# Three-pass split scores for the stick-breaking and the neighbourhood heads, with the sticks' low parts made on GpSimd

## The reference

```python
# stick-breaking: z = q k^T / 8, per block of 128 queries
log_beta = log_sigmoid(z)
log_1m = where(mask, log_sigmoid(-z), 0)
suffix = cumsum(log_1m, reverse) - log_1m
wts = where(mask, exp(log_beta + suffix), 0);  out = wts @ v
# neighbourhood: a grid of 8 rows by 64 columns; a query sees 16 columns of the 8 rows
p = softmax(q k^T / 8 + bias[row distance, column distance]);  out = p @ v
```

## Time and profile before

| | |
|---|---|
| runs | 1906.74, 1907.86, 1908.47 us, median 1907.86 |
| the profiled execution | 1907.13 us, span 1905.4 us from first to last instruction, mean granted clock 0.998 |
| TensorE, matmuls | 1890.5 us busy, 9126 instructions |
| DVE | 1072.6 us busy (56%) |
| ACT | 787.6 us busy (41%) |
| GpSimd | 159.3 us busy (8%) |
| stick stage | about 597 to 790 us from the start |
| neighbourhood stage | about 1539 to 1758 us |

### The profile page before, as it was taken

One profiled execution on the slowest core, in us unless ns is written; L12 is line 12 of the kernel. 1 busy time (PEld: TensorE's weight loads), 2 busy tenths in 40 slices (PEclk: granted clock), 3 DMA queues, 4 the chain that ended last, 5 costly groups with the idle time before them and its releaser, 6 DMA issues.

```text
span 1905.4 us, 25474 instructions
## 1 busy us (share of the span) xinstructions
PE 1890.5 (99%) x9126; PEld 1513.2 (79%) x9126; DVE 1072.6 (56%) x1719; ACT 787.6 (41%) x1261; POOL 159.3 (8%) x238
## 2 busy tenths in 40 slices
PE   9999999999999999999999999999999999999998
PEld 8888888888888777788888888876777887777777
DVE  7788534434456676654343446576676555655553
ACT  6576422222334444532222234255555344444442
POOL 3111000000000000000000000000002054532000
PEclk9999999999999999999999999999999999999999
DMA  7323332323232122223322232212313232322221
GB/s 249 115 93 121 100 98 91 114 84 99 95 100 77 60 66 66 79 91 97 110 99 82 94 111 88 67 45 62 95 56 92 83 95 79 91 78 89 77 93 68
DMA packets 50847, 173.78 MB, mean 91 GB/s; under 512 B 7456, under 2 KB 11680, under 8 KB 50768
## 3 DMA queue, kind: packets, MB, share of 16 engines
q1 hardware_dynamic: 44336, 162.62, 26.6%
q0 software_dynamic: 6432, 10.13, 2.1%
HBM read 168.51 MB, written 4.21 MB: 91 GB/s over the span
## 4 chain that ended last, share of the span: by engine, by line
PE 95%; DVE 2%; ACT 2%; issue 1%; DMA 1%; SPq 0%; DVEq 0%; ACTq 0%
PE ps L474 17%; PE ps L476 16%; PE ps L475 16%; PE sc L474 6%; PE sc L476 6%; PE sc L475 6%; PE tr L474 4%; PE tr L475 4%; PE tr L476 4%; PE ps L642 3%; PE tr L608 3%; PE sc L582 2%; PE ps L582 1%; PE sc L613 1%; PE ps L629 1%
## 5 line engine op out<-in xcount | busy, mean ns | idle before, releaser
L1020 ACT ACTIVATE Wh<-Wr 128x1024 fp32r<-128x1024 f32 (+2 forms) x268 | 300.2, 1120 | 642.6 <-PE ps L476 285.2
L474 PE MATMUL ps<-Hh,Wh 128*128 128x512 f32 x1136 | 465.7, 410 | 0.0
L476 PE MATMUL ps<-Hh,Wl 128*128 128x512 f32 x1136 | 444.3, 391 | 0.0
L475 PE MATMUL ps<-Hl,Wh 128*128 128x512 f32 x1136 | 443.1, 390 | 0.0
L1467 DVE TENSOR_TENSOR Wl<-Wr,Wh 128x1024 fp32r<-128x1024 f32 (+2 forms) x268 | 352.3, 1314 | 131.9 <-ACT Wh L1020 130.7
L474 PEld LDWEIGHTS ps<-Hh,Wh 128*128 128x128 f32 x1136 | 213.5, 188 | 56.8 <-issue 16.4
L476 PEld LDWEIGHTS ps<-Hh,Wl 128*128 128x128 f32 x1136 | 213.1, 188 | 47.0
L475 PEld LDWEIGHTS ps<-Hl,Wh 128*128 128x128 f32 x1136 | 213.9, 188 | 39.4 <-issue 0.5
L474 PE MATMUL sc<-Hh,Wh 128*128 128x512 f32 x432 | 168.6, 390 | 0.0
L475 PE MATMUL sc<-Hl,Wh 128*128 128x512 f32 x432 | 168.1, 389 | 0.0
L476 PE MATMUL sc<-Hh,Wl 128*128 128x512 f32 x432 | 168.1, 389 | 0.0
(11 more groups left out here) (307 smaller groups left out, 2639.7 us busy)
## 6 DMA issues: line engine op xcount, KB each, us to landing
Wr<-in_w SPq DMA_DIRECT2D x228, 512.0 KB, 3.5
Wr<-in_w SPq DMA_DIRECT2D x32, 768.0 KB, 4.3
Wr<-in_w SPq DMA_DIRECT2D x16, 640.0 KB, 3.9
scr<-in_rpb POOLq DMA_DIRECT2D x128, 24.0 KB, 2.1
X<-in_x SPq DMA_DIRECT2D x8, 256.0 KB, 4.4
Wr<-in_wri SPq DMA_DIRECT2D x4, 512.0 KB, 3.5
out_t<-X SPq DMA_DIRECT2D x8, 256.0 KB, 2.4
scr<-d_rel POOLq DMA_DIRECT2D x8, 192.0 KB, 3.6
```

What stands on the lines that cost most here:

```text
L474: pe.matmul(bank[:, 0:n], hi, rh[:, k, :], start=(k == 0), stop=False)
L475: pe.matmul(bank[:, 0:n], hi, rl[:, k, :], start=False, stop=False)
L476: return pe.matmul(bank[:, 0:n], lo, rh[:, k, :], start=False, stop=(k == kc - 1))
L1020: act.activation(place(Wh, slot, kc), place(Wr, slot, kc), ACT.Copy).then_inc(w_hi, 1)
```

## The change

1. Scores of the stick and neighbourhood pairs are split: for Q and K of the next pair there are high and low parts `Qh`, `Ql`, `Kh`, `Kl` in chunks 8 to 11 of `Yh` and `Yl`. ACT makes the high parts (`pair_hi`), 16 in each stage. The low parts are made by GpSimd for the sticks (a list of 16 in its program) and by DVE for the neighbourhood (`pair_lo`). `head` gets an argument `part`, and a chunk of scores is three products.
2. The group of scores is issued part by part, alternating between the heads; the 512-wide tile is one chunk; the wait on `nb_ok` stands behind the first part of head 0's wide tile.
3. At t = 0 TensorE waits for `qk_lo` in place of `taken`.
4. In `out_proj` of the sticks and of the recurrent block, units 4 and 5 come out of the loop and wait for the sums of units 0 and 1.
5. In the neighbourhood stage the last transposes go behind block 6 of unit 32, the last values behind block 1 of unit 33.

```diff
@@ -206,6 +206,8 @@
 
         QT, KT, VT, Vn = part(0, 2, S), part(1024, 2, S), part(2048, 2, S), part(3072, 2, S)
         Pb = part(4096, 4, S)
+        Qh, Ql, Kh, Kl = Yh[:, 8:10, :], Yl[:, 8:10, :], Yh[:, 10:12, :], Yl[:, 10:12, :]
+        pair_rows = {"q": (QT, Qh, Ql), "k": (KT, Kh, Kl), "qn": (QT, Qh, Ql), "kn": (KT, Kh, Kl)}
         PT = part(6144, 2, 4 * S)
         KT2 = part(10240, 2, S)
         ropes = part(11264, 2, S)
@@ -283,6 +285,7 @@
         t_s, t_nm, t_e, t_p, t_t, t_pt = (sem(n) for n in ("t_s", "t_nm", "t_e", "t_p", "t_t", "t_pt"))
         t_in, t_nr, nb_ok = sem("t_in"), sem("t_nr"), sem("nb_ok")
         t_av = sem("t_av")
+        qk_hi, qk_lo = sem("qk_hi"), sem("qk_lo")
         v_tp, v_ok = sem("v_tp"), sem("v_ok")
         sb_ok, yt_ok = sem("sb_ok"), sem("yt_ok")
         one_ok = sem("one_ok")
@@ -392,6 +395,13 @@
             for i in range(12, 16):
                 store_mem(i)
 
+            for n in range(8):
+                for tag in ("q", "k"):
+                    src, hi, lo = pair_rows[tag]
+                    pool.wait_ge(qk_hi, 2 * n + (1 if tag == "q" else 2))
+                    pool.tensor_tensor(lo[:, n % 2, :], src[:, n % 2, :], hi[:, n % 2, :].bitcast(F32), ALU.subtract)\
+                        .then_inc(qk_lo, 1)
+
             pool.wait_ge(t_p, STEP0["gqa"])
             pool.wait_ge(t_av, STEP0["gqa"] // 4)
             pool.dma_start(ropes, a["rope"]).then_inc(rope_in, 16)
@@ -525,7 +535,10 @@
                     if name == "rg_out":
                         unit(u0 + 2, CORNER, ps[2], kc, Yh, Yl)
                     unit(u0 + 3, 1, ps[3], kc, Yh, Yl)
-                    it0 = 2
+                    for m in range(2):
+                        pe.wait_ge(x_ok, x0 + m + 1)
+                        unit(u0 + 4 + m, m, ps[b0 + m], kc, Yh, Yl)
+                    it0 = 3
                 with pe.Fori(it0, 3 if name == "odd_out" else 4) as it:
                     for m in range(2):
                         pe.wait_ge(x_ok, 2 * it + (x0 + m - 1))
@@ -575,18 +588,38 @@
                 else:
                     wait(pe, t_e, g)
 
-                def head(t, h, c0, c1):
+                def head(t, h, c0, c1, part=None):
+
                     b, lo, hi = block_of(kind, t), 64 * h, 64 * h + 64
-                    k0 = key_chunks(kind, b)[0] * P
-                    keys = {GQA: KT[lo:hi, grp, c0:c1], WIN: KT2[lo:hi, grp, c0:c1]}.get(kind, KT[lo:hi, par, c0:c1])
-                    return pe.matmul(pair_bank(kind, t)[:, h, c0 - k0:c1 - k0], queries[lo:hi, b * P:(b + 1) * P], keys,
-                                     start=True, stop=True)
+                    k0, q = key_chunks(kind, b)[0] * P, slice(b * P, (b + 1) * P)
+                    out = pair_bank(kind, t)[:, h, c0 - k0:c1 - k0]
+                    if part is None:
+                        keys = {GQA: KT[lo:hi, grp, c0:c1], WIN: KT2[lo:hi, grp, c0:c1]}.get(kind, KT[lo:hi, par, c0:c1])
+                        return pe.matmul(out, queries[lo:hi, q], keys, start=True, stop=True)
+                    rows, keys = ((Qh, Kh), (Ql, Kh), (Qh, Kl))[part]
+                    return pe.matmul(out, rows[lo:hi, par, q], keys[lo:hi, par, c0:c1], start=(part == 0), stop=(part == 2))
 
                 def span(t):
                     cs = key_chunks(kind, block_of(kind, t))
                     return cs[0] * P, (cs[-1] + 1) * P
 
                 k0, k1 = span(t)
+                if kind in (STICK, NBR):
+                    for part in range(3):
+                        mm = head(t + 1, 0, *span(t + 1), part)
+                        if part == 2:
+                            mm.then_inc(nb_ok, 1)
+                        mm = head(t, 1, k0, k1, part)
+                    mm.then_inc(t_s, 2)
+                    for part in range(3):
+                        mm = head(t, 0, k0, k1, part)
+                        if part == 2:
+                            mm.then_inc(t_s, 2)
+                        if part == 0:
+                            pe.wait_ge(nb_ok, narrow)
+                        mm = head(t + 1, 1, *span(t + 1), part)
+                    mm.then_inc(nb_ok, 1)
+                    return
                 cuts = (k0, k0 + 256, k1) if k1 - k0 == S else (k0, k1)
                 if kind != GQA:
                     head(t + 1, 0, *span(t + 1)).then_inc(nb_ok, 1)
@@ -656,10 +689,10 @@
                     if k == 7:
                         mm.then_inc(w_used, 1)
 
-            def plain_units(name, first, n):
+            def plain_units(name, first, n, inside=None):
                 for q in range(first, first + n):
                     pe.wait_ge(taken, TAKEN0[name] + q - 1)
-                    unit(UNIT0[name] + q, q % 2, ps[q % 2])
+                    unit(UNIT0[name] + q, q % 2, ps[q % 2], after=inside if q == first else None)
 
 
             def mem_unit(u, bank, **kw):
@@ -764,7 +797,7 @@
                     for t in range(4):
                         g = 8 * i + (g0 + 2 * t)
                         if t == 0:
-                            pe.wait_ge(taken, nu * i + (tb + 2))
+                            pe.wait_ge(qk_lo, 2 * i + (2 if kind == STICK else 18))
                         if t % 2 == 0:
                             scores(kind, g, par, t, first=first and t == 0,
                                    narrow=4 * i + (2 * (t // 2) + (1 if kind == STICK else 49)))
@@ -815,15 +848,17 @@
                 pe.wait_ge(w_lo, u + 1)
                 for k in range(8):
                     mm = products(u % 2, ps[u % 2], k, KD, Hh, Hl, S)
-                    if k == 5:
+                    if k == (6 if kind == NBR else 5):
                         turn(kind, g - 2, 3)
                 mm.then_inc(w_used, 1)
-                values_pair(kind, g - 1, 1, o, grp, v_need)
+                if kind != NBR:
+                    values_pair(kind, g - 1, 1, o, grp, v_need)
 
             def mem_heads(seg, name, first_q, out):
                 early = seg == "mem0"
                 if not early:
-                    plain_units(name, first_q + 1, 3)
+                    last_values = lambda: values_pair(NBR, STEP0[seg] - 1, 1, OUT0[seg] - 1, 0, 26)
+                    plain_units(name, first_q + 1, 3, {1: last_values})
                 g0 = STEP0[seg]
                 for i in range(2):
                     for j in range(8):
@@ -1277,6 +1312,11 @@
                     wait(act, yt_ok, o)
                     act.activation(sg[:, :], gx[:, :], ACT.Tanh).then_inc(th_ok, 1)
 
+            def pair_hi(tag, t, par):
+                act.wait_ge(taken, t)
+                src, hi, _ = pair_rows[tag]
+                act.activation(hi[:, par, :], src[:, par, :], ACT.Copy).then_inc(qk_hi, 1)
+
             def square_head(r):
                 act.wait_ge(taken, TAKEN0["even_in"] + (1, 2, 4, 5, 6)[r])
                 wait(act, qa_ms, r - 1)
@@ -1291,11 +1331,16 @@
                 if kind == NBR:
                     act.activation(rf[:, :], ps[6][:, :], ACT.Copy, scale=DH ** -0.5).then_inc(rf_ok, 1)
                 split(ub + 3, 1, KD)
+                pair_hi(tags[0], tb + 1, 0)
+                pair_hi(tags[1], tb + 2, 0)
 
                 def pair(i, par, first, last):
                     n_pump = (0 if kind == STICK else 1) if last else nu
 
                     def pumped(j):
+                        for q in range(0 if last else 2):
+                            if (8 * q + 7) // nu + 1 == j:
+                                pair_hi(tags[q], nu * i + (tb + 3 + q + 1), 1 - par)
                         if last and kind == STICK and j == 1:
                             split(ub + 25, 1, KD)
                         if last and kind == STICK and j == 6:
@@ -1908,6 +1953,11 @@
                 elif tag == "raw":
                     dve.tensor_tensor(raw[par], bank, rt[:, :], ALU.mult).then_inc(taken, 1)
 
+            def pair_lo(tag, n, par):
+                dve.wait_ge(qk_hi, n)
+                src, hi, lo = pair_rows[tag]
+                dve.tensor_tensor(lo[:, par, :], src[:, par, :], hi[:, par, :].bitcast(F32), ALU.subtract).then_inc(qk_lo, 1)
+
             def pairs8(seg, kind, name, nu, y0, tags):
                 g0, o0, ub, tb = STEP0[seg], OUT0[seg], UNIT0[name], TAKEN0[name]
                 norm = "mix1" if kind == STICK else "odd"
@@ -1919,12 +1969,18 @@
                 take(tags[0], ub, 0)
                 take(tags[1], ub + 1, 1)
                 split(ub + 3, 1, KD)
+                if kind == NBR:
+                    pair_lo(tags[0], 17, 0)
+                    pair_lo(tags[1], 18, 0)
                 take(tags[2], ub + 2, 0)
 
                 def pair(i, par, first, last):
                     n_pump = (0 if kind == STICK else 1) if last else nu
 
                     def pumped(j):
+                        for q in range(0 if last or kind == STICK else 2):
+                            if (8 * q + 7) // nu + 2 == j:
```

(1 more changed line is left out.)

## The result

The changed kernel has a median of 1909.6 us over 17 runs (1908.4 to 1913.0), the kernel before one of 1906.75 over 17 (1905.7 to 1908.5): ratio 1.0015, 95% interval 1.0008 to 1.0022. That is 2.8 us more, where 2.3 less had been forecast. The profiled execution took 1909.93 us, span 1908.2.

What follows compares the result with a forecast made beforehand. TensorE, busy 1890.5 of 1905.4 us, was taken to bound the kernel. Terms -2.2 - 1.2 + 0.6 + 0.2 + 1.2 - 0.9 = -2.3 us gave 1904.8 profiled, median 1905.6; range 1901.0 to 1912.5.

Steps and rivals of the forecast that it cites:

- The step that failed: End of the neighbourhood stage: last values and transposes move by one or two products, no wait at either place, cost 0.
- If the neighbourhood stage gets a wait for a weight split: Stated sign of being wrong; the neighbourhood stage's added low parts on DVE were priced at 0, at most 0.5 per pair.
- V's transposes in the last stick pair: Stick pairs: V in SBUF near 671.6, its transposes after the group and three blocks, near 672.2, so cost 0.
- The 512 one: Stick groups of 512 and 256 keys: 1.34 against 1.49 us load to load, 8 times, a gain of 1.2 us.
- the 384 one: Stick groups of 384 and 128 keys: 1.15 against 1.07 us load to load, 8 times, a loss of 0.6 us.
- the neighbourhood groups: Score groups of 384 and 256 keys: 1.24 against 1.38 us, 16 times, gain 2.2 us, about 0.2 given back.
- rival 3: Narrow stick groups: 128-wide split parts run at the plain rate, 0.22 each; +3.1 us in all, median 1911.0; chance 0.08.
- rival 4: Score groups: weight loads of split parts in half-array rows are not hidden; +11.8 us in all, median 1919.7; chance 0.06.
- rival 2: K's low part in stick pairs: GpSimd loses the port to DVE, scores 1.9 late six times; +7.9, median 1915.8; chance 0.10.
- the wait of 0.25: Stick pairs' first scores wait for K's low part from GpSimd: 0.2 us in six pairs, a loss of 1.2 us.
- Rival 1: Score groups: parts behind nb_ok are not held up; -6.4 us in all, median 1901.5; chance 0.24.
- The output product: After the sticks, unit 4 waits for the first sum of X only, not the third: a gain of 0.9 us.

Runs made afterwards that it cites:

- experiments 1, 5: 1: changed kernel with last values and turn back, 1906.4 us; 5: changed kernel, only turn one product earlier, 1909.1, or unit 33's weights split before gate's tanh, 1906.5.
- experiment 8: Changed kernel with two blocks of the output product put in front of V's transposes and the turn in the last stick pair: 1909.3 us, ratio 1.0011.
- experiment 6: Changed kernel with the wait for nb_ok, and head 1's narrow parts, behind all three parts of head 0's wide tile: 1907.9 us, ratio 1.0004.

## Why the prediction was wrong

**The step that failed.** "The last values and the transposes in front of them move by one or two products; no wait stands at either place, so 0." It asked whether TensorE had waited at the old and the new place, not what the moved work had covered. The 2.3 us of values stood between unit 32 and unit 33, whose weights ACT and DVE were splitting until 1770.01, and with them gone 2.34 us of wait stand there (experiments 1, 5). With the half clock, which came in this execution and not in all, this is 4.2 us of the profiled one, more than the change's whole loss. "If the neighbourhood stage gets a wait for a weight split" was named as a way to be wrong; it came, though not from DVE's added low parts.

**V's transposes in the last stick pair.** "Its transposes come after the group and three blocks, near 672.2, so 0": the delay of V was nearly right (1.2 forecast, 1.1 measured), and the cover too for seven pairs. The last pair pumps no products, and there it cost 1.0 (experiment 8). The term was priced on a running pair and not on the last.

**The stick groups.** The 512 one was forecast at 1.34 and took 1.47, the 384 one at 1.15 and took 1.22: together +1.0 us where -0.6 had been forecast. The mechanism was right: the parts queued behind `nb_ok` are held up (experiment 6). The time at which the waiting load can go was mis-sized. It was taken from the end of the narrow parts alone (0.68, and 0.60 for 128 keys). But the load goes into head 1's half of the array, which is busy with its wide parts until 0.81 at 512 columns (0.11 + 3 x 0.23) and 0.62 at 384. The load came at 0.81, and at 0.68 in both groups with 384, though the last narrow part's record ends 0.07 earlier where the parts are 128 wide. That the load waits for its own half is read from these distances; no run varied it alone. So the agreement in the neighbourhood groups (forecast 1.24, measured 1.22) was right in size and not wholly for its reason.

**What held.** 128-wide parts follow each other by 0.11, a load's time (657.63, .74, .85): rival 3 is out, and so is rival 4, since loads of the same row group lie under running products. GpSimd won the port (rival 2 is out): K's low parts take 1.29, and the wait of 0.25 was forecast at 0.2. Rival 1 (-6.4) did not come. The output product gained 0.9, as forecast:

```profile
803.41 0.39 PE L486 MATMUL sc<-Yh,Wl 128*128 128x512 f32 x1
...
803.64 0.39 PE L484 MATMUL ps<-Yh,Wh 128*128 128x512 f32 x1
```

0.23 apart, where a wait of 0.62 stood. The Trainium skill's rule on the port ("SBUF — State Buffer", "Who interferes with whom") is what the last stick pair shows, DVE held for 1.1 us by a GpSimd instruction that had begun 0.03 before it. The Trainium skill's rule that loads overlap running products only across row groups ("TensorE: Matmul & The Clock Gate", Part 3) is not borne out by the split parts either: in one half of the array they follow each other by 0.12 us (1657.40 to 1657.52), each with a load of 0.11.

## What to carry to other kernels

Before work is moved on the engine that bounds the kernel, list what runs on the other engines beneath it and who needs that next: a place without a wait may be one that hides two others. Price a repeated step in its last and first repetition too, where the products that cover it are missing. Where a part is added to a chain of an engine without slack, another engine doesn't help if it takes its turn in the same chain; an earlier place, in an idle stretch, does.

## What the runs showed of the hardware

- A wait of 2.34 us of a TensorE that was busy before it was followed by 3.4 us at 1.2 GHz in four of six traces, beginning 0 to 1.3 us behind its end, and by none in two; one of 1.65 us was not, in the one trace that has it. The half clock cost 1.6 us each time, two thirds of the wait itself. By the mean granted clocks it came in 19 or more of 72 executions. What decides between the executions is open.
- Three split parts of 128 columns in one half of the array follow each other by 0.11 us, the time of their loads (657.52 to 657.85); at 256 it is 0.12, at 384 0.17, at 512 0.23.
- A load for one half of the array that waits for a semaphore did not start while that half was still streaming, though loads without a wait do (at 657.63, behind a product of 384 columns begun at 657.52): in the group with 512 keys it came at 0.81, when the half's last product ended; in the groups with 384 keys it came 0.06 us after the half's last product.
